# A two-layer block on one core: the end of the embedding gate, the blockwise inverse and the leads of one feed-forward are changed

## The chip, the cores and the metric

The kernel runs on one core of a Trainium2 chip. The metric is the device time of one execution in microseconds (us); lower is better. A core has five engines that each work through a queue of their own in order: TensorE (PE, matrix products and transposes), VectorE (DVE), ScalarE (ACT), GpSimd (POOL) and SyncE (SP, here the issuer of nearly all loads). They meet through semaphores. SBUF is the working memory, PSUM the memory of eight banks into which PE writes.

## The reference

The input is 256 tokens of 1024 columns. A first block of two layers is followed by a second block of two. The changed parts lie in the first block, and at the output of the second:

```python
def swiglu(x, w_in, w_out):
    gate, up = jnp.split(x @ w_in, 2, axis=-1)
    return (jax.nn.silu(gate) * up) @ w_out
...
    # token_mix, delta rule in chunks of 64 tokens, 4 heads
    m = jnp.where(strict, jnp.einsum('nbhik,nbhjk->nbhij', k_beta, k) * decay, 0.0)
    eye = jnp.eye(CHUNK, dtype=m.dtype)
    t_inv = lax.linalg.triangular_solve(eye + m, jnp.broadcast_to(eye, m.shape),
                                        left_side=True, lower=True)
    u = jnp.einsum('nbhij,nbhjv->nbhiv', t_inv, v * beta[..., None])
    w = jnp.einsum('nbhij,nbhjk->nbhik', t_inv, k_beta * jnp.exp(gcum)[..., None])
...
    # first_block
    for i in range(DEPTH):
        x = layer_norm(ALPHA * x + 0.5 * swiglu(x, ffn_w_in[i, 0], ffn_w_out[i, 0]), ln_g[i, 0], ln_b[i, 0])
        mix = token_mix(x, mix_w_in[i], ...)
        x = layer_norm(ALPHA * x + mix, ln_g[i, 1], ln_b[i, 1])
        x = layer_norm(ALPHA * x + 0.5 * swiglu(x, ffn_w_in[i, 1], ffn_w_out[i, 1]), ln_g[i, 2], ln_b[i, 2])
        ple = jax.nn.sigmoid(x @ ple_w_gate[i] + ple_b_gate[i]) * (p[i] @ ple_w_proj[i])
        x = layer_norm(ALPHA * x + ple, ln_g[i, 3], ln_b[i, 3])
```

There are 16 inverses of 64x64 in each layer (4 chunks of 64 tokens, 4 heads). The second block ends each of its layers with a product by `w_out` and a layer norm.

## The kernel before

**Products.** All data are fp32. A product is made of three on PE: high by high, high by low, low by high, where the high part is the operand rounded on ACT and the low part is the rest. Weights come in chunks of 1024 columns through six raw buffers (`raw`); ACT rounds a chunk into one of eight buffers `WH` (L312), then DVE or POOL subtracts and writes the low part `rawL` (L315). `round_chunk` and `pump` put these steps into the queues of ACT, DVE and POOL at the place in the program where they are called, so the order of the code is the order of the queues; a chunk used as an operand is asked for five chunks ahead. The activations, two halves of 128 tokens (t = 0, 1), are normalised rows `xt`, which PE turns (L597) into PSUM; ACT rounds them to `xTH` and DVE subtracts to `xTL` (`ln_split`).

**Phases.** Each layer of the first block goes through `ffn`, `mix`, `ffn`, `ple`. Each phase is a generator: `end_phase` runs the last product of one phase, its layer norm, and lets the generator of the next (`next(nxt)`) start its first products on half 0 (the *lead* units: their chunks hold four k of 256 columns, 12 tile products of 128x256, or two k of 512 columns) while half 1 is still being normalised.

**The end of a phase.** `by_tokens` makes the last product in steps of one k and one piece of columns: first three k for all pieces, then the rest of each piece. `inside` holds what is emitted ahead of a step: rounding and splits (`splits`), the layer norm of half 0 (`norm`) and its transposes (`turn`). For `ple` the second half has three pieces (512, 256 and 256 columns), 24 steps, and the sums and statistics follow piece by piece. The steps of `inside` are written by hand:

```python
inside = {0: norm, 6: splits} if not slow else {6: lambda: (splits(), norm())}
inside.update({first: lambda: turn(0, 0, x0), first + 1: lambda: turn(0, 1, x0)})
```

`slow` is set by `ple` alone, with `first` = 18; ACT must load a table of functions for the sigmoid and one for the square root of the layer norm (L334).

**The inverse** in `mix`: U, the inverse of 16 blocks, and its transpose T are built in five levels from masked blocks B of the matrix (`Bs`, masks made on POOL). A level makes Z = B U (products U, B in the trace), then U -= T-products and T -= Z-products:

```python
p = pe([Z_ready[t], T_ready[t], free], blocks(t, b, T, Z))
U_ready[t] = tt(half(U, t), half(U, t), half_ps(b, t), ALU.subtract, [p])
```

`blocks` walks over the blocks with two of the array's 64x64 quadrants in turn. Between these short products `go(n)` puts pieces of the next weight product on PE (12 tile products of 128x256 each), and `aside_` the convolution (`conv_steps`), `decayed_q`, `k_tokens` and `v_tokens`, which work on DVE and partly with transposes on PE (L1256). The products by the finished inverse follow (L1359 and what is behind it); the latter half of those walks over four quadrants in turn.

Of the kernel before, what the change touches and what calls it, by code (L numbers as in the profile page):

```python
# [24 lines left out]
S = 256  # L25
# [16 lines left out]

PHASES = [p for l in range(DEPTH) for p in (("ffn", l, 0), ("mix", l), ("ffn", l, 1), ("ple", l))]
# [5 lines left out]
def weight_units(phases):  # L49
# [14 lines left out]
    for ph in phases:  # L64
        l = ph[1]
        if ph[0] == "ffn":
            j = ph[2]
            for f in range(2):
# [3 lines left out]
            for f in range(2, NF):  # L72
# [173 lines left out]
def program(nc, io, phases=PHASES):  # L246
# [253 lines left out]

    def by_tokens(us, ks, t, aH, aL, a_ready, first, end, free, inside={}, place=None):
# [25 lines left out]
    def row_product(keys, order, aH, aL, a_ready, after={}):  # L527

        nu = len(order) // 2
        free = [bank_free[b] for b in range(4, 8)]  # L530
        for g in range(nu - LAST):
            u = Unit(keys + (g,))
            for i in range(2):
                k, first = order[2 * g + i], g == 0 and i == 0

                def fn(e, u=u, i=i, k=k, first=first):
                    for t in range(2):
                        for n in range(2):
                            e.matmul(PS[:, 4 + 2 * t + n, :], aH(k, t), u.H(i, 512 * n, 512), start=first, stop=False)  # L539
                            e.matmul(PS[:, 4 + 2 * t + n, :], aH(k, t), u.L(i, 512 * n, 512), start=False, stop=False)  # L540
                        for n in range(2):
                            ins = e.matmul(PS[:, 4 + 2 * t + n, :], aL(k, t), u.H(i, 512 * n, 512), start=False, stop=False)  # L542
# [6 lines left out]
        return lambda t, inside={}: by_tokens(us, order[2 * (nu - LAST):], t, aH, aL, a_ready, nu == LAST, True, free, inside)  # L549
# [10 lines left out]

    quarters_at = [None]
    quarter = [None]
# [45 lines left out]
    def add_acc(per):  # L608

        def fn(t, n, tok):  # L610
            yn, b = xt[:, t, 512 * n:512 * n + 512], 4 + 2 * t + n
            return stt(PS[:, b, :], yn, ALPHA * per, PS[:, b, :], ALU.mult, ALU.add, [tok, xt_loaded])
        return fn

    def end_phase(products, total, eps, nxt, first=9, slow=False):
# [9 lines left out]
        if nxt is None:  # L625
            x0 = ln_apply(0, stats, eps)
            last = products(1)
            x1 = ln_apply(1, [ln_stats(1, n, total(1, n, last[n, 0])) for n in range(2)], eps)
            for t, xs in ((0, x0), (1, x1)):
                for n in range(2):  # L630
# [27 lines left out]
        inside = {0: norm, 6: splits} if not slow else {6: lambda: (splits(), norm())}  # L658
        inside.update({first: lambda: turn(0, 0, x0), first + 1: lambda: turn(0, 1, x0)})
# [20 lines left out]
        for n in range(2):  # L680
# [3 lines left out]
            pump(st["split"])  # L684
# [7 lines left out]
    def ffn(l, j, nxt, start):  # L692
# [4 lines left out]
        sl, hl_ = take(f"sl{l}{j}", [128, 2, 2, 128]), take(f"hl{l}{j}", [128, 2, 2, 128])  # L697

        us = [Unit(("ffn_lead", l, j, f)) for f in range(2)]
        lead_h = {}
        lead_bank = {}
        lead_tok = {}

        def lead(t, f, c):
            if t not in lead_bank:
                lead_bank[t] = bank("A")
            b, free = lead_bank[t]
            n = KD // len(us[f].k)  # L710

            def fn(e):
                for q in range(n):
                    k = n * c + q
                    ins = mm3_moving(e, PS[:, b, 256 * f:256 * f + 256], xTH[:, k, 128 * t:128 * t + 128], xTL[:, k, 128 * t:128 * t + 128],
# [1446 lines left out]
```

How the kernel before makes its waits and increments, by code:

```python
    def play(self, handle, name):  # L222
        seen = {}
        for waits, fn, sem, inc in self.entries[name]:
            for s, v in waits:
                if seen.get(s.name, 0) < v:
                    seen[s.name] = v
                    handle.wait_ge(s, v)
            ins = fn(handle)
            if sem is not None:
                ins.then_inc(sem, inc)
# [1849 lines left out]
        @block.sync  # L2081
        def _(e):
            Q.play(e, "sync")
            e.wait_ge(sem_out, Q.loads[sem_out.name])
```

## Time and profile before

| | us |
|---|---|
| median of 3 runs | 1531.83 (1531.14 to 1532.82) |
| the profiled execution | 1531.08, its span 1529.3 |
| PE busy in the span | 1510.0 (99%) |
| DVE / ACT / POOL busy | 958.5 / 810.3 / 238.9 |
| mean granted clock of PE | 0.996 |
| read from HBM | 263.46 MB, 173 GB/s |

The span runs from the first to the last instruction that the profiler shows. Busy shares are means over stages of very different kinds: which engine sets the time has to be read at each place, from what PE waits for there. A clock of 1.00 is 2.4 GHz, 0.50 is 1.2 GHz.

### The profile page before, as it was taken

Reading aid. Unit: us, or ns where it says so; the run is one execution under the profiler, and the core shown is the slowest. Engines: PE = TensorE matmul, PEld = TensorE weight load, DVE = VectorE, ACT = ScalarE, POOL = GpSimd, SP = SyncE. Lnnn points to the kernel's source line nnn. Section 1 sums busy time; section 2 is a strip of 40 time slices with the busy share of each in tenths; the row PEclk is TensorE's granted clock in tenths of the full one; section 3 lists DMA queues with packets and bytes.
Section 4 is the critical chain, followed back from the end, with each engine's and each line's share of the span. In section 5 each row is a group of like instructions: output and inputs, shape, how many; then the busy total and the mean of one; then the engine's idle time right before and its main releaser. Section 6 shows DMA issues by size and latency. Waiting matters only on the chain.

```text
span 1529.3 us, 27766 instructions
## 1 busy us (share of the span) xinstructions
PE 1510.0 (99%) x11812; PEld 1396.0 (91%) x11812; DVE 958.5 (63%) x1389; ACT 810.3 (53%) x1249; POOL 238.9 (16%) x135
## 2 busy tenths in 40 slices
PE   9999999999999999999999999999999999999997
PEld 8998899989998879998899989998779999899996
DVE  6555476676555466654558685655476766767756
ACT  6544375545544355544574554544465675555762
POOL 0000242113000240000431040000420004500041
PEclk9999999999999999999999999999999999999999
DMA  9655463136555456555543155555455334553341
GB/s 384 220 193 193 166 221 130 66 111 224 190 193 193 165 203 217 193 193 193 196 164 112 56 175 211 193 193 192 165 184 190 136 115 161 206 194 138 118 159 56
DMA packets 39579, 266.30 MB, mean 174 GB/s; under 512 B 4444, under 2 KB 4444, under 8 KB 9248
## 3 DMA queue, kind: packets, MB, share of 16 engines
q1 hardware_dynamic: 38160, 260.13, 47.8%
q0 software_dynamic: 720, 3.35, 0.5%
q8 instruction: 94, 1.54, 0.4%
q10 hardware_dynamic: 576, 1.05, 0.2%
q14 instruction: 29, 0.24, 0.0%
HBM read 263.46 MB, written 1.05 MB: 173 GB/s over the span
## 4 chain that ended last, share of the span: by engine, by line
PE 94%; DVE 3%; ACT 1%; DMA 0%; issue 0%; POOL 0%; SPq 0%; DVEq 0%
PE PS L483 17%; PE PS L484 17%; PE PS L485 17%; PE PS L497 6%; PE PS L499 6%; PE PS L498 6%; PE PS L539 4%; PE PS L542 4%; PE PS L540 4%; PE PS L1270 2%; PE PS L466 1%; PE PS L467 1%; PE PS L468 1%; PE PS L1850 1%; PE PS L597 1%; DVE rawL L315 1%
## 5 line engine op out<-in xcount | busy, mean ns | idle before, releaser
L483 PE MATMUL PS<-xTH,WH 128*128 128x256 f32 x2272 | 645.8, 284 | 0.0
L484 PE MATMUL PS<-xTL,WH 128*128 128x256 f32 x2272 | 633.2, 279 | 0.0
L485 PE MATMUL PS<-xTH,rawL 128*128 128x256 f32 x2272 | 631.1, 278 | 0.0
L312 ACT ACTIVATE WH<-raw 128x1024 fp32r<-128x1024 f32 (+2 forms) x476 | 484.2, 1048 | 127.4 <-PE PS L542 101.3
L315 DVE TENSOR_TENSOR rawL<-raw,WH 128x1024 fp32r<-128x1024 f32 (+1 forms) x400 | 488.5, 1249 | 98.0 <-ACT WH L312 97.7
L483 PEld LDWEIGHTS PS<-xTH,WH 128*128 128x128 f32 x2272 | 426.7, 188 | 9.2 <-issue 6.7
L484 PEld LDWEIGHTS PS<-xTL,WH 128*128 128x128 f32 x2272 | 426.5, 188 | 3.4 <-issue 2.9
L485 PEld LDWEIGHTS PS<-xTH,rawL 128*128 128x128 f32 x2272 | 428.1, 188 | 0.0
L315 POOL TENSOR_TENSOR rawL<-raw,WH 128x1024 fp32r<-128x1024 f32 (+1 forms) x76 | 184.4, 2447 | 1069.1 <-ACT WH L312 1069.1
L312 ACT ACTIVATE sg<-PS 128x256 f32<-128x256 f32 x80 | 30.7, 384 | 182.4 <-PE PS L485 182.4
L315 DVE TENSOR_TENSOR hh<-PS,sg 128x256 f32<-128x256 f32 x80 | 33.9, 424 | 147.5 <-ACT sg L312 147.5
L539 PE MATMUL PS<-WH,hTH 128*128 128x512 f32 x256 | 100.7, 393 | 0.0
L540 PE MATMUL PS<-rawL,hTH 128*128 128x512 f32 x256 | 100.4, 392 | 0.0
L497 PE MATMUL PS<-WH,xTH 128*128 128x256 f32 (+2 forms) x272 | 89.2, 328 | 4.8 <-DVE rawL L315 2.4
L498 PE MATMUL PS<-rawL,xTH 128*128 128x256 f32 (+2 forms) x272 | 86.3, 317 | 0.0
L499 PE MATMUL PS<-WH,xTL 128*128 128x256 f32 (+2 forms) x272 | 86.2, 317 | 0.0
L542 PE MATMUL PS<-WH,hTL 128*128 128x512 f32 x256 | 79.9, 393 | 0.0
L318 DVE SCALAR_TENSOR_TENSOR PS<-xt,PS 128x512 f32<-128x512 f32 (+1 forms) x42 | 28.2, 671 | 61.9 <-PE PS L499 61.1
L497 PEld LDWEIGHTS PS<-WH,xTH 128*128 128x128 f32 x272 | 51.8, 191 | 10.9 <-ACT xTH L312 3.2
L315 DVE TENSOR_TENSOR hTL<-hh,hTH 128x256 fp32r<-128x256 f32 x80 | 34.1, 426 | 38.8 <-ACT hTH L312 38.8
L542 PEld LDWEIGHTS PS<-WH,hTL 128*128 128x128 f32 x256 | 48.1, 188 | 11.0
L539 PEld LDWEIGHTS PS<-WH,hTH 128*128 128x128 f32 x256 | 48.1, 188 | 10.8
(357 smaller groups left out, 2009.4 us busy)
## 6 DMA issues: line engine op xcount, KB each, us to landing
raw<-in_weights SPq DMA_DIRECT2D x233, 1024.0 KB, 4.8
gb<-in_lngb SPq DMA_DIRECT2D x16, 512.0 KB, 5.4
raw<-in_weights SPq DMA_DIRECT2D x2, 1056.0 KB, 4.9
gb<-in_ln SPq DMA_DIRECT2D x4, 512.0 KB, 4.3
cst<-in_consts POOLq DMA_DIRECT2D x1, 1378.5 KB, 10.3
raw<-in_weights SPq DMA_DIRECT2D x4, 256.0 KB, 5.4
x0T<-in_xT ACTq DMA_DIRECT2D x4, 256.0 KB, 5.7
xt<-in_x POOLq DMA_DIRECT2D x1, 1024.0 KB, 16.6
```

What stands on the lines that cost most here:

```text
L312: return Q.put("act", waits, lambda e: e.activation(out, in_, func, **kw))
L315: return Q.put(eng, waits, lambda e: e.tensor_tensor(out, a, b, op))
L483: e.matmul(out, c, xTH[:, k, :], start=k == 0, stop=False)
L484: e.matmul(out, c, xTL[:, k, :], start=False, stop=False)
L485: ins = e.matmul(out, u.L(i, 128 * k, 128), xTH[:, k, :], start=False, stop=k == KD - 1)
L497: e.matmul(out, aH, u.H(i, c0, w), start=first, stop=False)
L498: e.matmul(out, aH, u.L(i, c0, w), start=False, stop=False)
L499: return e.matmul(out, aL, u.H(i, c0, w), start=False, stop=end)
L539: e.matmul(PS[:, 4 + 2 * t + n, :], aH(k, t), u.H(i, 512 * n, 512), start=first, stop=False)
L540: e.matmul(PS[:, 4 + 2 * t + n, :], aH(k, t), u.L(i, 512 * n, 512), start=False, stop=False)
L542: ins = e.matmul(PS[:, 4 + 2 * t + n, :], aL(k, t), u.H(i, 512 * n, 512), start=False, stop=False)
L1270: ins = e.matmul(PS[R, b, 64 * i:64 * i + 64], lhsT[R, i, :], rhs[R, i, :], start=True, stop=True)
```

## The change

It has five parts.

1. **End of the embedding gate** (`end_phase` with `slow`): ACT's table for the square root is loaded ahead of rounding; rounding and splits are emitted ahead of steps 3, 6 and 9, not at step 6 alone; half 0's transposes stand ahead of steps 14 and 16, not 18 and 19. In layer one (`extra`) the table for half 1 and another round of splits on POOL come ahead of the first lead products, and later splits go to POOL too.
2. **Third lead unit** in layer two's first feed-forward (`lead_units`): three units instead of two run ahead, both halves of the third share a bank (`third_tok`, `third_act`), and its activations need two more transposes (`hl3`).
3. **First products of the program** (`lead_parts`): on half 0 each of the three products by parts waits for its own operand only.
4. **The inverse**: T is no longer updated with products; each level turns U with four full transposes (`flip`) and copies the result to T on DVE. Products of Z and of U run over the four quadrants in turn into two banks (`quadrants`); U is updated in two strided halves.
5. **End of the program**: the last row product of half 1 is made in three pieces (512, 256, 256), summed and normalised piece by piece; half 0 is stored as soon as it is ready, and the last stores are of 256 columns.

The core of the diff (allocation and renaming of the bank bookkeeping cut):

```diff
+def lead_units(l, j):
+    return 3 if l > 0 and j == 0 else 2
...
-    def row_product(keys, order, aH, aL, a_ready, after={}):
+    def quarters(where):
+        quarters_at[0] = where
+        quarter[0], free = bank("A")
+        return {(0, 0, 512): PS[:, 6, :], (1, 0, 256): PS[:, 7, 0:256], (1, 256, 256): PS[:, quarter[0], 0:256]}, free
...
-    def end_phase(products, total, eps, nxt, first=9, slow=False):
+    def end_phase(products, total, eps, nxt, first=(9, 10), slow=False, extra=False):
...
-            x0 = ln_apply(0, stats, eps)
+            def store(t, c0, w, tok):
+                src, dst = xt[:, t, c0:c0 + w], io["out"][128 * t:128 * t + 128, c0:c0 + w]
+                Q.dma("sync", [tok], sem_out, lambda e: e.dma_start(dst, src))
+            for n, tok in enumerate(ln_apply(0, stats, eps)):
+                store(0, 512 * n, 512, tok)
             last = products(1)
-            x1 = ln_apply(1, [ln_stats(1, n, total(1, n, last[n, 0])) for n in range(2)], eps)
-            for t, xs in ((0, x0), (1, x1)):
-                for n in range(2):
-                    src = xt[:, t, 512 * n:512 * n + 512]
-                    dst = io["out"][128 * t:128 * t + 128, 512 * n:512 * n + 512]
-                    Q.dma("sync", [xs[n]], sem_out, lambda e, src=src, dst=dst: e.dma_start(dst, src))
+            y = total(1, 0, last[0, 0])
+            stats = [ln_stats(1, 0, y, part) for part in range(2)]
+            stats += [ln_stats(1, 1, total(1, 1, last[1, 256 * part], c0=256 * part, w=256), part) for part in range(2)]
+            x1 = ln_apply(1, stats, eps)
+            store(1, 0, 512, x1[0])
+            for part in range(2):
+                store(1, 512 + 256 * part, 256, x1[1][part])
             return
+        if slow:
+            table(TBL_SQRT)
...
-        inside = {0: norm, 6: splits} if not slow else {6: lambda: (splits(), norm())}
-        inside.update({first: lambda: turn(0, 0, x0), first + 1: lambda: turn(0, 1, x0)})
+        inside = {0: norm, 6: splits} if not slow else {3: splits, 6: lambda: (splits(), norm()), 9: splits}
+        inside.update({first[0]: lambda: turn(0, 0, x0), first[1]: lambda: turn(0, 1, x0)})
...
             quarter_sum(0)
             pump(st["split"], "pool", lead=0)
             quarter_sum(1)
+            if extra:
+                table(TBL_SQRT)
+                pump(st["split"], "pool", lead=0)
...
-            pump(st["split"])
+            pump(st["split"], "pool" if extra else None)
...
+            key, col = (t, 256 * f) if f < 2 else ("third", 256 * t)
...
+            w, x = us[f].ready(c, 0), xT_ready[t][n * c // 4]
+            if start and t == 0:
+                tok = lead_parts(us[f], f, c, n, w, x, PS[:, b, 256 * f:256 * f + 256], free)
+            else:
+                tok = pe([w, x, free], fn)
+            (lead_tok if f < 2 else third_tok)[t] = tok
...
+        def lead_parts(u, f, c, n, w, x, out, free):
+            toks = []
+            for part in range(3):
+                def fn(e, part=part):
+                    for q in range(n):
+                        k = n * c + q
+                        a, b = (xTL if part == 1 else xTH)[:, k, 0:128], (u.L if part == 2 else u.H)(c, 256 * q, 256)
+                        ins = e.matmul(out, a, b, start=part == 0 and k == 0 and f == 0, stop=part == 2 and k == KD - 1 and f == 1)
+                    return ins
+                toks.append(pe([[w[0], x[0], free], x[1], w[1]][part], fn))
+            return toks[-1]
...
+        def third_act():
+            b, _ = lead_bank["third"]
+            v = PS[:, b, :].rearrange("p (t g s) -> p t g s", t=2, g=2)
+            s = act(sl3[:, :, :], v[:, :, 0, :], ACT.Silu, [third_tok[0], third_tok[1]])
+            lead_h[2] = tt(hl3[:, :, :], v[:, :, 1, :], sl3[:, :, :], ALU.mult, [s])
+            release(b, lead_h[2])
...
-            for f, c in ((0, 0), (0, 1), (1, 0)):
+            for f, c in ((0, 0), (0, 1), (1, 0)) + (((1, 1),) if nl == 3 else ()):
...
-            lead(0, 1, 1)
+            lead(0, *((2, 0) if nl == 3 else (1, 1)))
...
+        if nl == 3:
+            lead(0, 2, 1)
...
+                if nl == 3:
+                    b, free = bank("A")
+                    def fn(e, b=b):
+                        for t in range(2):
+                            ins = e.transpose(PS[:, b, 128 * t:128 * t + 128], hl3[:, t, :], ident)
+                        return ins
+                    p = pe([lead_h[2], free], fn)
+                    h_ready[2] = split(hTH[:, 2, :], hTL[:, 2, :], PS[:, b, 0:S], [p])
+                    release(b, h_ready[2])
...
-        end_phase(products, total, "eps5x4", nxt, 18, True)
+        end_phase(products, total, "eps5x4", nxt, (14, 16), True, l + 1 < DEPTH)
...
+        def quadrants(bs, lhsT, rhs, back):
+            def fn(e):
+                for m in range(4):
+                    for a_, odd in ((0, 0), (1, 1), (0, 1), (1, 0)):
+                        i, c, R, O = 2 * m + odd, 2 * m + a_, slice(64 * a_, 64 * a_ + 64), slice(64 * odd, 64 * odd + 64)
+                        out, src, j, b = (R, O, c, bs[odd]) if back else (O, R, i, bs[a_])
+                        ins = e.matmul(PS[out, b, 64 * m:64 * m + 64], lhsT[src, j, :], rhs[src, j, :], start=True, stop=True)
+                return ins
+            return fn
+        def flip(b, x):
+            def fn(e):
+                for m in range(4):
+                    ins = e.transpose(PS[:, b, 128 * m:128 * m + 128], x[:, 2 * m:2 * m + 2, :].rearrange("p i s -> p (i s)"), ident)
+                return ins
+            return fn
...
-        T_ready = [tt(half(T, t), eye, half(Bs[0], t), ALU.subtract, [b_ready[0]]) for t in range(2)]
...
         for n in range(1, 6):
             B = Bs[n % 2]
+            b, free = bank("B")
+            p = pe([U_ready, free], flip(b, U))
+            T_ready = copy(T[:, :, :], PS[:, b, :].rearrange("p (i s) -> p i s", i=8), [p])
+            release(b, T_ready)
             zb_ = [bank("B") for _ in range(2)]
+            p = pe([b_ready[n], U_ready, [free for _, free in zb_]], quadrants([b for b, _ in zb_], B, U, False))
             Z_ready = []
-            for t in range(2):
-                b, free = zb_[t]
-                p = pe([b_ready[n], U_ready[t], free], blocks(t, b, B, U))
-                Z_ready.append(act(half(Z, t), half_ps(b, t), ACT.Copy, [p]))
-                release(b, Z_ready[t])
+            for k, (b, _) in enumerate(zb_):
+                Z_ready.append(act(every2(Z, k), every2_ps(b), ACT.Copy, [p]))
+                release(b, Z_ready[k])
             b_free[n % 2] = p
             if n + 2 < 6:
                 level_mask(n + 2)
             go(1)
             if n == 5:
                 v_tokens(1)
-            for t in range(2):
-                b, free = bank("B")
-                p = pe([Z_ready[t], T_ready[t], free], blocks(t, b, T, Z))
-                U_ready[t] = tt(half(U, t), half(U, t), half_ps(b, t), ALU.subtract, [p])
-                release(b, U_ready[t])
-                if n < 5:
-                    b, free = bank("B")
-                    p = pe([free], blocks(t, b, Z, T))
-                    T_ready[t] = tt(half(T, t), half(T, t), half_ps(b, t), ALU.subtract, [p])
-                    release(b, T_ready[t])
+            ub = [bank("B") for _ in range(2)]
+            p = pe([Z_ready, T_ready, [free for _, free in ub]], quadrants([b for b, _ in ub], T, Z, True))
+            for k, (b, _) in enumerate(ub):
+                U_ready[k] = tt(every2(U, k), every2(U, k), every2_ps(b), ALU.subtract, [p])
+                release(b, U_ready[k])
```

On ACT's queue at the end of layer one's embedding gate, from the sigmoids of half 0 on (`PS<-PS` are the sigmoids, `lnsd` the square root, `xTH` half 0's rounded rows, `WH` weight chunks), stood before:

```order
L312 ACTIVATE PS<-PS 128x512 x2
L312 ACTIVATE WH4_64<-raw5_59 128x1024
L312 ACTIVATE WH5_65<-raw5_59 128x1024
L334 ACT_TABLE_LOAD
L312 ACTIVATE lnsd_78<-lnmv_77,cst_49 128x1
L334 ACT_TABLE_LOAD
L312 ACTIVATE xTH_52<-PS 128x4x128
L312 ACTIVATE PS<-PS 128x512
L312 ACTIVATE xTH_52<-PS 128x4x128
L312 ACTIVATE PS<-PS 128x256
L312 ACTIVATE WH6_66<-raw0_54 128x1024
L312 ACTIVATE PS<-PS 128x256
```

and stand now:

```order
L316 ACTIVATE PS<-PS 128x512 x2
L338 ACT_TABLE_LOAD
L316 ACTIVATE WH4_64<-raw5_59 128x1024
L316 ACTIVATE WH5_65<-raw5_59 128x1024
L316 ACTIVATE lnsd_78<-lnmv_77,cst_49 128x1
L338 ACT_TABLE_LOAD
L316 ACTIVATE WH6_66<-raw0_54 128x1024
L316 ACTIVATE xTH_52<-PS 128x4x128
L316 ACTIVATE PS<-PS 128x512
L316 ACTIVATE xTH_52<-PS 128x4x128
L316 ACTIVATE PS<-PS 128x256
L316 ACTIVATE WH7_67<-raw0_54 128x1024
```

The first table load has moved ahead of two roundings, and `WH6` ahead of half 0's rows; `WH7` now stands between the sigmoids, where `WH6` stood.

On PE at the same place, where half 1's first transposes (`cst,xt`, the identity and the rows) come between lead products, stood before:

```order
L497 MATMUL PS<-WH6_66,xTH_52 128x256
L498 MATMUL PS<-rawL0_68,xTH_52 128x256
L499 MATMUL PS<-WH6_66,xTL_53 128x256
L597 MATMUL PS<-cst_49,xt_51 128x128 x4
L497 MATMUL PS<-WH7_67,xTH_52 128x256
L498 MATMUL PS<-rawL0_68,xTH_52 128x256
L499 MATMUL PS<-WH7_67,xTL_53 128x256
```

and stand now:

```order
L501 MATMUL PS<-WH7_67,xTH_52 128x256
L502 MATMUL PS<-rawL0_68,xTH_52 128x256
L503 MATMUL PS<-WH7_67,xTL_53 128x256
L614 MATMUL PS<-cst_49,xt_51 128x128 x4
L501 MATMUL PS<-WH0_60,xTH_52 128x256
L502 MATMUL PS<-rawL1_69,xTH_52 128x256
L503 MATMUL PS<-WH0_60,xTL_53 128x256
```

The transposes now stand behind the chunk `WH7`, and the next chunk, `WH0`, is the third unit's.

On DVE in the inverse of layer one, from the U of level 1 to that of level 2, stood before (`cva` are convolution steps, `eb` belongs to `decayed_q`):

```order
L315 TENSOR_TENSOR U0_109<-U0_109,PS 128x256
L315 TENSOR_TENSOR T0_108<-T0_108,PS 128x256
L315 TENSOR_TENSOR U0_109<-U0_109,PS 128x256
L315 TENSOR_TENSOR T0_108<-T0_108,PS 128x256
L315 TENSOR_TENSOR rawL3_71<-raw3_57,WH4_64 128x1024
L318 SCALAR_TENSOR_TENSOR cva0_94<-PS,par_50,cva0_94 128x255 x2
L318 SCALAR_TENSOR_TENSOR cva0_94<-PS,par_50,cva0_94 128x254 x2
L315 TENSOR_TENSOR eb0_100<-eb0_100,kq0_93 128x512
L315 TENSOR_TENSOR U0_109<-U0_109,PS 128x256
```

and stand now, from the copy of level 1 to that of level 2:

```order
L328 COPY T0_110<-PS 128x512
L319 TENSOR_TENSOR U0_111<-U0_111,PS 128x4x64 x2
L319 TENSOR_TENSOR rawL3_71<-raw3_57,WH4_64 128x1024
L322 SCALAR_TENSOR_TENSOR cva0_96<-PS,par_50,cva0_96 128x255 x2
L322 SCALAR_TENSOR_TENSOR cva0_96<-PS,par_50,cva0_96 128x254 x2
L319 TENSOR_TENSOR eb0_102<-eb0_102,kq0_95 128x512
L328 COPY T0_110<-PS 128x512
```

The four halves of U and T have become one copy ahead of two strided halves of U; the second copy stands behind split, convolution and `eb`.

## Rows read from the trace of the kernel before

**Rows 1.** The page: the chain that ended last, by engine

```profile
PE 94%; DVE 3%; ACT 1%; DMA 0%; issue 0%; POOL 0%; SPq 0%; DVEq 0%
```

**Rows 2.** Windows, PE alone: stretch, us, busy, rows, clock, DMA share, GB/s

```profile
562.24:572.32 10.08, 7.10 (x59) 1.00 0.79 317
572.32:578.05 5.73, 5.73 (x52) 1.00 0.72 219
1120.57:1127.94 7.37, 5.22 (x24) 1.00 0.95 389
1127.94:1134.85 6.91, 6.05 (x17) 0.51 0.54 183
1134.85:1137.86 3.01, 3.01 (x14) 1.00 0.19 27
```

**Rows 3.** Timeline, layer one's embedding end: start, length, engine, operation, [idle <-releaser]

```profile
559.24 0.60 PE L597 MATMUL PS<-cst,xt 128*128 128x128 f32 x4
...
559.60 0.36 PE L497 MATMUL PS<-WH,xTH 128*128 128x256 f32 x1
...
560.51 0.69 DVE L315 TENSOR_TENSOR xTL<-PS,xTH 128x512 fp32r<-128x512 f32 x1 [1.48 <-ACT xTH L312]
...
561.67 1.05 ACT L312 ACTIVATE WH<-raw 128x1024 fp32r<-128x1024 f32 x1
...
563.01 1.28 ACT L334 ACT_TABLE_LOAD   x1
...
566.35 0.26 DVE L576 BATCH_NORM_AGGREGATE lnmv<-lnq 128x2 f32<-128x24 f32 x1
...
567.97 2.35 POOL L315 TENSOR_TENSOR rawL<-raw,WH 128x1024 fp32r<-128x1024 f32 x1 [2.77 <-ACT WH L312]
...
568.72 0.66 PE L597 MATMUL PS<-cst,xt 128*128 128x128 f32 x4 [1.77 <-DVE xt L318]
...
570.47 0.36 PE L497 MATMUL PS<-WH,xTH 128*128 128x256 f32 x1 [1.09 <-POOL rawL L315]
```

**Rows 4.** Timeline, layer two's embedding end

```profile
1127.04 0.66 PE L597 MATMUL PS<-cst,xt 128*128 128x128 f32 x4 [1.80 <-DVE xt L318]
```

**Rows 5.** Windows, layer one's inverse: PE, weight load, DVE, ACT, POOL; clock, DMA, GB/s

```profile
255.33:287.55 32.22, 32.22 (x585) 30.09 (x584) 24.44 (x45) 11.55 (x22) 4.98 (x6) 1.00 0.27 97
```

**Rows 6.** Chain, layer one's inverse: start, length, engine, line, rows

```profile
258.06 2.01 PE PS L1270 x64
...
293.33 0.62 PE PS L1359 x32
```

**Rows 7.** Timeline, layer one's inverse and just behind it, PE, DVE and POOL

```profile
261.59 1.65 DVE L318 SCALAR_TENSOR_TENSOR cva<-PS,par,cva 128x255 f32<-128x255 f32 x4
...
262.86 1.30 POOL L315 TENSOR_TENSOR Ba<-Es,cst 128x512 f32<-128x512 f32 x1 [4.99 <-PE PS L1270]
...
263.15 1.55 DVE L315 TENSOR_TENSOR eb<-eb,kq 128x512 f32<-128x512 f32 x1
...
264.99 0.42 DVE L315 TENSOR_TENSOR U<-U,PS 128x256 f32<-128x256 f32 x1 [0.28 <-PE PS L1270]
...
266.73 1.22 DVE L315 TENSOR_TENSOR rawL<-raw,WH 128x1024 fp32r<-128x1024 f32 x1
...
267.76 0.60 PE L1256 MATMUL PS<-cst,kq 128*128 128x128 f32 x4
...
268.29 1.15 PE L1270 MATMUL PS<-U,Bb 64*64 64x64 f32 x32
...
269.37 0.38 PE L483 MATMUL PS<-xTH,WH 128*128 128x256 f32 x1
...
297.50 0.68 DVE L324 COPY Sa<-PS 128x512 f32<-128x512 f32 x1
```

**Rows 8.** Timeline, the program's start

```profile
5.66 1.13 ACT L312 ACTIVATE WH<-raw 128x512 fp32r<-128x512 f32 x2
...
7.23 0.36 PE L497 MATMUL PS<-WH,xTH 128*128 128x256 f32 x1 [1.77 <-DVE rawL L315]
```

More of the change, by code:

```diff
@@ L67, in weight_units @@
             j = ph[2]
-            for f in range(2):
+            for f in range(lead_units(l, j)):
                 n = 4 if units else 2
@@ L71, in weight_units @@
                                                        for kt in range(n * c, n * c + n)] for c in range(KD // n)]))
-            for f in range(2, NF):
+            for f in range(lead_units(l, j), NF):
                 tile_unit(("ffn_in", l, j, f), "ffn_w_in", (l, j), t(128 * f), t(DFF + 128 * f))
@@ L499, in mm3_moving @@
         return e.matmul(out, aL, u.H(i, c0, w), start=False, stop=end)
+    quarters_at = [None]
+    quarter = [None]
     def by_tokens(us, ks, t, aH, aL, a_ready, first, end, free, inside={}, place=None):
@@ L525, in program, with row_product @@
     LAST = 3
-    def row_product(keys, order, aH, aL, a_ready, after={}):
+    def quarters(where):
+        quarters_at[0] = where
+        quarter[0], free = bank("A")
+        return {(0, 0, 512): PS[:, 6, :], (1, 0, 256): PS[:, 7, 0:256], (1, 256, 256): PS[:, quarter[0], 0:256]}, free
+    def row_product(keys, order, aH, aL, a_ready, after={}, quarters_in=None):
         nu = len(order) // 2
         free = [bank_free[b] for b in range(4, 8)]
+        place = None
+        if quarters_in is not None:
+            place, freeq = quarters(quarters_in)
+            free.append(freeq)
         for g in range(nu - LAST):
@@ L537, in fn @@
                     for t in range(2):
-                        for n in range(2):
[L539 to L542, printed above, removed]
+                        pieces = {(n, 0, 512): PS[:, 4 + 2 * t + n, :] for n in range(2)}
+                        if t == 1 and place:
+                            pieces = place
+                        for (n, c0, w), out in pieces.items():
+                            e.matmul(out, aH(k, t), u.H(i, 512 * n + c0, w), start=first, stop=False)
+                            e.matmul(out, aH(k, t), u.L(i, 512 * n + c0, w), start=False, stop=False)
+                        for (n, c0, w), out in pieces.items():
+                            ins = e.matmul(out, aL(k, t), u.H(i, 512 * n + c0, w), start=False, stop=False)
                     return ins
@@ L548, in row_product @@
         us = [Unit(keys + (nu - LAST + q,)) for q in range(LAST)]
-        return lambda t, inside={}: by_tokens(us, order[2 * (nu - LAST):], t, aH, aL, a_ready, nu == LAST, True, free, inside)
+        return lambda t, inside={}: by_tokens(us, order[2 * (nu - LAST):], t, aH, aL, a_ready, nu == LAST, True, free, inside, place if t else None)
     aside = []
@@ L697, in ffn @@
         sl, hl_ = take(f"sl{l}{j}", [128, 2, 2, 128]), take(f"hl{l}{j}", [128, 2, 2, 128])
-        us = [Unit(("ffn_lead", l, j, f)) for f in range(2)]
+        sl3, hl3 = take(f"sl3{l}{j}", [128, 2, 128]), take(f"hl3{l}{j}", [128, 2, 128])
+        nl = lead_units(l, j)
+        us = [Unit(("ffn_lead", l, j, f)) for f in range(nl)]
         lead_h = {}
@@ L747, in ffn @@
             for c in range(2):
-                for f in range(2):
+                for f in range(nl):
                     lead(1, f, c)
@@ L751, in ffn @@
         lead_act(1)
+        if nl == 3:
+            third_act()
         h_ready = {}
         h_tok = {}
-        for f in range(2, NF):
+        for f in range(nl, NF):
             u = Unit(("ffn_in", l, j, f))
@@ L833, in ple @@
         bgR, *bias_ready = ple_bias[l]
-        quarters_at[0] = at(f"lnq{l}", [128, 4, 6], F32, over + PLE_AT + 13 * 1024)
+        lnq = at(f"lnq{l}", [128, 4, 6], F32, over + PLE_AT + 13 * 1024)
         def aH(k, t):
```

36 lines of the change are left out of this document (19 added, 17 removed).

## Prediction

> **What bounds the kernel now.** The chain that ended last comes first [rows 1]: 94% of it is TensorE (PE). So a term counts only if it takes products or transposes off PE, or takes away time in which PE waits or runs slowly; what DVE, ACT and POOL save where PE never stops is worth nothing. The second view is a table of chosen stretches for PE alone, at the ends of the two embedding gates (ple) [rows 2]. Layer one: from the first lead product on token half 0 to the first unit on both halves, PE needs 10.08 us for 48 products of 128x256 and two sets of four transposes. The next stretch of 5.73 holds 48 products too (its 52 rows take in some that reach over its edges): 0.119 each, 0.36 for a step of three; a set of transposes takes 0.36 (559.24 to the next row at 559.60) [rows 3]. That is 6.4, so 3.65 us are lost. Layer two: 7.37 + 6.91 = 14.28 us for 30 products of 128x512, of which the row after shows 13 in 3.01 (0.232 each): 6.95 + 0.7, so 6.63 are lost. There the granted clock is 0.51 from 1127.94 on, the 1.2 GHz level, after PE had waited twice; 12 products and a set of transposes lie in it, 3.1 us of work at 2.4 GHz that took 6.05. So 2.9 of the 6.63 are clock, 3.7 waiting. The rows of the two ends name the waits: 1.77 and 1.80 for the normalised rows of token half 1 (xt), 1.09 for a low part of weights made on POOL [rows 3, 4]. In the block inverse, by contrast, PE is busy for all of 32.22 us in each layer [rows 5]: there it is work that must go, not waiting.
>
> **The embedding's end.** DVE works without a pause from the first split of half 0 (560.51) to the last aggregate (566.35 + 0.26), and the transposes of half 1's x follow at 568.72, 2.1 us later [rows 3]. The start of that DVE stretch hangs on half 0's transposes, which stand before step 18 of 24 (559.24). They move to step 14, four steps of 0.36 earlier, so the stretch starts 1.4 us sooner, and with it all that follows. Between 0 and 1.4 is possible, since the last quarter of half 1's gate cannot come sooner than its last product at 562.24; I take 1.4, because DVE has most of its work on the earlier pieces. The early table of half 0 takes a load of 1.28 off ACT's path, but PE did not wait there: nothing.
>
> Layer one: after the gate's last product there are now four lead chunks of 12 products (4 x 1.43 = 5.7) instead of three ahead of half 1's transposes: until 567.95, while x is there at 568.72 - 1.4 = 567.3. So the wait of 1.77 goes (bound: some of it stays, if x is late). Next come a chunk of the third unit (1.43), the other transposes, and its second chunk, wanted at 567.95 + 0.36 + 1.43 + 0.36 = 570.1. Low parts: the chunk that waited 1.09 is now rounded one slot earlier, so it has no wait. The third unit's first rounding follows a table load that ends at 563.01 + 1.28 = 564.3 and takes 1.05; then POOL has two splits of 2.35 in a row, to 570.1 [rows 3]. So 0.1 to 0.2 of waiting is left, and its two transposes on PE are new, some 0.2. Gain **3.3** (bounds: 1.9 if POOL is most of a split late, 3.6). The third unit's products are only moved.
>
> Layer two has no third unit. Its 18 lead products end at 1120.57 + 18 x 0.232 = 1124.75, x arrives at 1127.04 - 1.4 = 1125.6 (0.9 lost) [rows 2, 4], the last chunk now has its low part, and half 1's own splits behind the transposes I allow 0.5, most of a split of 0.69 [rows 3]. Loss 1.4 instead of 3.7, and no two long waits in a row, so I expect no fall of the clock: layer one had the same two waits and stayed at 1.00 [rows 2, 3]. Gain 2.3 + 2.9 = **5.2** (bounds: 2.3 with the fall kept, 6.0).
>
> **The inverse.** Before, a level costs PE 1.08 us for its first 16 products (two rows each in the trace) and 2.01 for the 32 others (T and U); the fifth level has 16 of those [rows 6, 7]. After, T is U turned by four full transposes and copied by DVE, and both sets of 16 go over four quadrants in turn. Products in just that order stand in the trace: 16 in 0.62 [rows 6]. Four transposes in this stage take 0.53 (267.76 to 268.29) [rows 7]. A level then costs 0.53 + 2 x 0.62 = 1.77. Sum: 4 x 3.09 + 2.16 = 14.5 before, 5 x 1.77 = 8.85 after, 5.7 us per layer if PE stays busy.
>
> But PE will not stay busy, because of who is in front of the T copy. It stands on DVE behind the previous level's U, the weight split and that level's aside work, and the second set of products waits for it. From rows [rows 7], level 1 to 2: two U 0.84, split 1.22, four convolution steps 1.65, one product on eb 0.68 (as the copy of 128x512; it took 1.55 beside POOL's mask), T copy 0.68; less 0.3, since each row starts a little before the one ahead ends: 4.8. Then PE's 0.62 and two hand-overs of 0.15: 5.7, and with part of eb's overlap 6.2. PE alone could do the level in two runs of twelve tile products (1.43, and 0.17 for the change of kind, as 0.53 against 0.36 shows for transposes) and 1.77, 4.97. Levels 2 to 3 (two steps, two passes of 0.68) and 3 to 4 (four steps, two passes) come to 5.6 and 6.4 in the same way, and 4 to 5 to 6.0, where PE with its own extra transposes is the longer. With 3.6 ahead of the first U and 1.4 behind the last: 29.2 against 32.22 [rows 5]. Gain 2.9 per layer, **5.8** (bounds: 0 per layer, if every level meets a busy DVE at the wrong moment; 5.7).
>
> POOL's mask lasts 1.30 in that stage [rows 7]; no row shows a copy from PSUM beside POOL. SBUF — State Buffer in the Trainium skill, section Who interferes with whom, says that DVE copies and GpSimd can shut each other out of the shared port for a whole instruction. By that rule one T copy per layer would wait for the rest of a mask, and the sum would be 2 x 0.6 smaller.
>
> **Start and end of the program.** The first product waits 1.77 us until a low part is done; in three parts, the first needs only ACT's rounded part, finished at about 6.2, half way through 5.66 + 1.13 [rows 8]. The whole chunk still needs the low part, so a chunk ends only about 0.5 sooner, and the next half's x is not earlier: gain **0.3** (0 to 0.6). At the end, the sum and the statistics of the last 512 columns become those of 256: passes of 0.42 instead of 0.68 [rows 7], two of them, **0.5** (0 to 1.0). The early stores and the smaller pieces in PE's last row product I put at nothing: PE takes 0.119 for 256 columns against 0.232 for 512.
>
> **Sum.** 3.3 + 5.2 + 5.8 + 0.3 + 0.5 = 15.1. The profiled execution took 1531.08, so 1516.0; its time is 0.75 below the median 1531.83, so I say **1516.7**.
>
> **Rivals.** (a) The clock still falls once, at an embedding's end or in the new inverse with its short waits: 2.9 to 3.4 worse, 1520. For it: two equal ends gave one fall and one not. Against: waits now much shorter. 0.15. (b) DVE is no limit in the inverse, because convolution steps slip into PE's longer stretches: 5.7 per layer, 1511. For it: DVE is busy 24.4 of 32.2 us there [rows 5]. Against: the order on its queue. 0.12. (c) The inverse gives nothing, T's copy returning all that the quadrants save: 1522.5. 0.10. (d) Slower than before: PE runs at 1.2 GHz in the inverse, where its work gets thinner and has waits in it. The 26.5 us of products per layer would double: 53 more, 1570 if in all of it. From 15 of those 53, when PE is at that level for more than three tenths of the stage, the change loses. Against: in the old inverse the clock is 1.00 throughout [rows 5]. 0.02. TensorE: Matmul & The Clock Gate in the Trainium skill, section Why this matters for your kernels, warns of idle gaps between bursts. (e) The change does not act at the ends: PE's waits belong to something else there, as the landing of weights; 1525 with the inverse alone. 0.03.
>
> **How the numbers follow.** My forecast has 0.58, with a range of its own of 1513.5 to 1519. To leave out no more than two in ten I take in (a), (b) and the near side of (c): **1511 to 1521.5**. What differs by less than 0.2% (3 us) cannot be told from no change here. Only (d) and far ends of (c) and (e) come near that: faster 0.95, same 0.03, slower 0.02.
>
> **What will show it.** Right: at both ends the waits of 1.77 to 1.80 shrink below 1.0 or vanish, and no stretch at half clock follows; sets of 32 small product rows at 0.62; the inverse's stretch at 29 us, with PE waits of about a microsecond ahead of the second set in the middle levels, and T's copy as the releaser. Wrong: a stretch of 26.5 (b) or of 32 (c); a granted clock of 0.5 inside the inverse (d); the sets over quadrants still at 1.08, which would take away 4.6 us of PE's saving per layer.

## The result and the profile after

| | before | changed |
|---|---|---|
| median, us | 1532.32 (1531.14 to 1533.93, 4 runs) | 1514.78 (1514.39 to 1514.95, 4 runs) |
| profiled execution, us | 1531.08 | 1514.83 |
| its span | 1529.3 | 1513.0 |

The ratio is 0.9886, with a 95% interval of 0.9872 to 0.9901: faster by 1.1%. The forecast was 1516.7, its range 1511 to 1521.5.

The page's chain that ended last, by engine, beside [rows 1]: PE still carries it.

```profile
PE 94%; DVE 4%; ACT 1%; DMA 0%; issue 0%; SPq 0%; DVEq 0%
```

The view of waits for PE says what is left (engine, line and what it waited for; us in total, times, longest):

```profile
PE PS L1351 <- DVE T L328: 4.3, 4, 1.1
PE PS L2131 <- DVE warm L2127: 1.2, 1, 1.2
PE PS L470 <- DVE mt L322: 0.7, 1, 0.7
PE PS L614 <- DVE xt L322: 0.7, 1, 0.7
```

The wait for T's copy (L328) is new, twice in each layer. At the embeddings' ends only one wait of 0.7 is left. The same view of the kernel before has 5.8 us there:

```profile
PE PS L597 <- DVE xt L318: 3.6, 2, 1.8
...
PE PS L497 <- POOL rawL L315: 2.2, 2, 1.1
```

The windows of the two ends, PE alone, columns as in [rows 2]. The first holds layer one's six lead chunks on half 0 (72 products) and the two sets of transposes; the other two hold layer two's 30 products and two sets:

```profile
557.98:567.41 9.43, 9.43 (x82) 1.00 0.92 356
1109.27:1114.32 5.05, 4.34 (x20) 1.00 0.88 371
1114.32:1118.30 3.98, 3.98 (x21) 1.00 0.88 363
```

Layer one's stretch is 9.43 us without idle time for 72 products (1.43 per chunk, 8.6) and two sets. Layer two's 14.28 are 9.03, and the clock is 1.00 throughout. The timeline at both ends shows why (rows between are left out):

```profile
554.84 0.69 DVE L319 TENSOR_TENSOR xTL<-PS,xTH 128x512 fp32r<-128x512 f32 x1 [1.00 <-ACT xTH L316]
...
560.68 0.26 DVE L593 BATCH_NORM_AGGREGATE lnmv<-lnq 128x2 f32<-128x24 f32 x1
563.64 0.60 PE L614 MATMUL PS<-cst,xt 128*128 128x128 f32 x4
...
1114.32 0.66 PE L614 MATMUL PS<-cst,xt 128*128 128x128 f32 x4 [0.71 <-DVE xt L322]
```

DVE's stretch is as long as before (554.84 to 560.94, 6.10 us; 560.51 to 566.61 in [rows 3]), but the last aggregate ends 3.0 us after the gate's last product (557.98) instead of 4.4: 1.4 sooner, as forecast.

In the inverse (all engines, columns as in [rows 5]) the stretch from the first transposes of U to the first product with v is

```profile
254.78:283.31 28.53, 26.39 (x479) 23.95 (x477) 22.27 (x40) 11.36 (x22) 4.96 (x6) 1.00 0.29 108
```

26.39 us of work, 2.13 of idle time. The timeline takes 0.69 for a set of 32 small rows and 1.15 for one of before [rows 7]; the chain's view, which the forecast's 0.62 and 1.08 come from, has a set begin 0.07 later. The timeline from the second set of level 1 to that of level 4, DVE, POOL and the second sets:

```profile
257.51 0.69 PE L1351 MATMUL PS<-Z,T 64*64 64x64 f32 x32
258.28 0.75 DVE L319 TENSOR_TENSOR U<-U,PS 128x256 f32<-128x256 f32 x2 [2.17 <-PE PS L1351]
258.95 1.22 DVE L319 TENSOR_TENSOR rawL<-raw,WH 128x1024 fp32r<-128x1024 f32 x1
260.08 1.65 DVE L322 SCALAR_TENSOR_TENSOR cva<-PS,par,cva 128x255 f32<-128x255 f32 x4
261.01 1.29 POOL L319 TENSOR_TENSOR Ba<-Es,cst 128x512 f32<-128x512 f32 x1 [3.60 <-PE PS L1351]
261.64 1.21 DVE L319 TENSOR_TENSOR eb<-eb,kq 128x512 f32<-128x512 f32 x1
262.77 0.68 DVE L328 COPY T<-PS 128x512 f32<-128x512 f32 x1
263.60 0.69 PE L1351 MATMUL PS<-Z,T 64*64 64x64 f32 x32 [1.14 <-DVE T L328]
...
267.49 1.29 POOL L319 TENSOR_TENSOR Bb<-Es,cst 128x512 f32<-128x512 f32 x1 [5.18 <-PE PS L1351]
268.13 0.68 DVE L328 COPY T<-PS 128x512 f32<-128x512 f32 x1
268.95 0.69 PE L1351 MATMUL PS<-Z,T 64*64 64x64 f32 x32
...
275.34 0.69 PE L1351 MATMUL PS<-Z,T 64*64 64x64 f32 x32 [0.99 <-DVE T L328]
```

DVE runs from 258.28 to 263.45 without a pause, and PE's second set starts 0.15 behind the copy.

Where the time went, by the starts of the same PE instructions in the two traces (each gain is the difference of the two stretches):

| stretch | forecast | measured |
|---|---|---|
| start, to the first product of q and k | 0.3 | 0.33 |
| layer one, inverse | 2.9 | 3.92 |
| layer one's end and layer two's first feed-forward | 3.3 | 3.13 |
| layer two, inverse | 2.9 | 3.93 |
| layer two's end | 5.2 | 5.22 |
| second block, up to its last row product | 0 | -0.76 |
| last row product and end | 0.5 | 0.49 |
| sum | 15.1 | 16.26 |

The sum is the difference of the two profiled executions' spans; the medians lie 17.5 apart.

### The profile page after: what moved, and what is told of

It is laid out like the page before. It is cut to its first block, busy times and chain, and to the rows that moved or that the text cites. A ratio compares the mean times of both kernels' runs of the same rounds, so it can differ in the third digit from the quotient of the medians.

```text
span 1513.0 us, 27372 instructions
## 1 busy us (share of the span) xinstructions
PE 1496.9 (99%) x11622; PEld 1384.2 (91%) x11622; DVE 947.8 (63%) x1379; ACT 811.1 (54%) x1249; POOL 250.5 (17%) x140
## 4 chain that ended last, share of the span: by engine, by line
PE 94%; DVE 4%; ACT 1%; DMA 0%; issue 0%; SPq 0%; DVEq 0%
PE PS L487 17%; PE PS L488 17%; PE PS L489 16%; PE PS L501 6%; PE PS L503 6%; PE PS L502 6%; PE PS L559 4%; PE PS L562 4%; PE PS L560 4%; PE PS L470 1%; PE PS L471 1%; PE PS L472 1%; PE PS L614 1%; PE PS L1942 1%; DVE rawL L319 1%; PE PS L1351 1%
## 5 line engine op out<-in xcount | busy, mean ns | idle before, releaser
L487 PE MATMUL PS<-xTH,WH 128*128 128x256 f32 x2256 | 641.2, 284 | 0.0
L319 DVE TENSOR_TENSOR rawL<-raw,WH 128x1024 fp32r<-128x1024 f32 (+1 forms) x395 | 481.4, 1245 | 102.5 <-ACT WH L316 102.2
L487 PEld LDWEIGHTS PS<-xTH,WH 128*128 128x128 f32 x2256 | 423.6, 188 | 9.2 <-issue 6.7
L319 POOL TENSOR_TENSOR rawL<-raw,WH 128x1024 fp32r<-128x1024 f32 (+1 forms) x81 | 196.1, 2443 | 1049.8 <-ACT WH L316 1049.8
L560 PEld LDWEIGHTS PS<-rawL,hTH 128*128 128x128 f32 x256 | 48.1, 188 | 10.7
```

The source lines that it names most:

```text
L319: return Q.put(eng, waits, lambda e: e.tensor_tensor(out, a, b, op))
L487: e.matmul(out, c, xTH[:, k, :], start=k == 0, stop=False)
L560: e.matmul(out, aH(k, t), u.L(i, 512 * n + c0, w), start=False, stop=False)
```

## The experiments

Each kernel is the changed one with one edit, beside runs of the kernel before on the same chip.

**1. The inverse of before.** The section from the first U to the end of a level is exchanged:

```diff
-            p = pe([U_ready, free], flip(b, U))
-            T_ready = copy(T[:, :, :], PS[:, b, :].rearrange("p (i s) -> p i s", i=8), [p])
...
+                    p = pe([free], blocks(t, b, Z, T))
+                    T_ready[t] = tt(half(T, t), half(T, t), half_ps(b, t), ALU.subtract, [p])
```

> All of the change except the inverse, which is that of before (T updated by products, two quadrants in turn). The theory: the new inverse gives 3.9 us in each layer, by how far the products ahead of it and behind it stand apart in the two traces, so this kernel takes 7.9 more than the changed one, about 1522.7, its stretch is 32.2 us again, and the ends of the two embeddings look as in the changed kernel. The rival: part of that shift comes from the neighbours (the next weights' low parts, the third lead unit), and this kernel costs less than 5 us more, under 1519.8.

Measured: 1522.21 (1521.62 to 1522.64), ratio 0.9945 (0.9931 to 0.9960); the stretch is 32.22 us again, and the ends look as in the changed kernel. So the inverse is worth 7.4 us by the medians (of runs on two chips) and 7.8 by the profiled executions; the rest of the change is worth 8.4, by the runs of the kernel before beside these (1530.61).

**2. T's copy on ACT.**

```diff
-            T_ready = copy(T[:, :, :], PS[:, b, :].rearrange("p (i s) -> p i s", i=8), [p])
+            T_ready = act(T[:, :, :], PS[:, b, :].rearrange("p (i s) -> p i s", i=8), ACT.Copy, [p])
```

> The changed kernel with the copy of T on ACT instead of DVE. The theory: the waits of 1.14 and 0.99 us ahead of the second set of products in levels 2 and 4 come from what stands ahead of the copy on DVE's queue (U, split, convolution, eb). On ACT only the previous rounding stands there, so these waits go: 2.1 us per layer, 4.3 in all, about 1510.5. The rival: the copy is late because the transposes are, or ACT's own copies of Z now come 0.6 later and take the same time back: within 1 us of the changed kernel, 1513.8 to 1515.8.

Measured: 1509.83 (1509.10 to 1510.18), ratio 0.9864 (0.9848 to 0.9881). The window of all engines over the same stretch:

```profile
254.93:281.12 26.19, 26.19 (x478) 23.87 (x477) 19.18 (x35) 14.14 (x27) 4.97 (x6) 1.00 0.32 118
```

No idle time on PE: the stretch is the PE work alone, 2.3 us shorter. The wait belonged to DVE's queue. The two versions were timed again side by side:

> The changed kernel as it is, beside the next one on the same chip: 1514.8, within 0.5, with the same waits of 0.95 to 1.14 in levels 2 and 4. All theories say so.

> The kernel with T's copy on ACT as it is, beside the changed kernel on the same chip. The theory of DVE's queue: 4.3 to 5 less than the changed kernel, 1510. The rival, that the first comparison owed part of its difference to two chips: less than 3 between them.

Measured: 1514.96 (1514.07 to 1515.46), ratio to before 0.9894 (0.9877 to 0.9911), and 1510.47 (1509.94 to 1510.64), ratio 0.9866 (0.9849 to 0.9882). 4.5 us apart: this version beats both.

**3. Half 0's transposes late again.**

```diff
-        end_phase(products, total, "eps5x4", nxt, (14, 16), True, l + 1 < DEPTH)
+        end_phase(products, total, "eps5x4", nxt, (18, 19), True, l + 1 < DEPTH)
```

> The changed kernel with half 0's transposes ahead of steps 18 and 19 again at both embeddings' ends; rounding ahead of steps 3, 6 and 9 stays. The theory: the start of DVE's stretch hangs on these transposes, so half 1's rows come 1.4 us later. In layer two the wait of 0.71 becomes 2.1 and the clock may fall again (2.9 more); in layer one the lead products end at the time the rows came before, and 1.3 of waiting comes back. Together 2.7 more, or 5.6 with the fall: 1517.5 or 1520.4. The rival: DVE waits for the last pieces of the gate anyway, and the place of the transposes is worth less than 0.5: 1514.8 to 1515.3.

Measured: 1517.39 (1516.52 to 1519.09), ratio 0.9916 (0.9901 to 0.9930). The timeline at both ends, and the window of PE behind the second:

```profile
564.60 0.65 PE L614 MATMUL PS<-cst,xt 128*128 128x128 f32 x4 [0.68 <-DVE xt L322]
...
1116.68 0.66 PE L614 MATMUL PS<-cst,xt 128*128 128x128 f32 x4 [2.13 <-DVE xt L322]
```

```profile
1116.68:1121.23 4.55, 4.54 (x17) 0.62 0.71 219
```

The wait of 0.71 is 2.13, as expected, and the clock falls behind it; layer one gets 0.68 where 1.3 was expected. By the traces layer one's end costs 0.87 more and layer two's 2.75, of which 1.42 are waiting; the rest, 1.3, is the fall, for which 2.9 was expected.

**4. Rounding ahead of step 6 alone.**

```diff
-        inside = {0: norm, 6: splits} if not slow else {3: splits, 6: lambda: (splits(), norm()), 9: splits}
+        inside = {0: norm, 6: splits} if not slow else {6: lambda: (splits(), norm())}
```

> The changed kernel with rounding and splits emitted ahead of step 6 alone, as before; the transposes stay at steps 14 and 16, the early table stays. The theory: the wait of 1.1 us for POOL's low part comes back in layer two, and in layer one each of the lead chunks' low parts is a slot later, so that one wait of 1 to 1.4 us stands there too: 2.2 more, 1517.0, more by 2.9 if the clock falls with it. The rival: POOL has time to spare once half 1's rows come sooner, and nothing changes: 1514.8.

Measured: 1517.90 (1517.69 to 1519.97), ratio 0.9921 (0.9906 to 0.9935). The timeline of PE at the two ends:

```profile
563.75 0.36 PE L501 MATMUL PS<-WH,xTH 128*128 128x256 f32 x1 [1.15 <-POOL rawL L319]
...
566.08 0.36 PE L501 MATMUL PS<-WH,xTH 128*128 128x256 f32 x1 [0.25 <-POOL rawL L319]
...
568.44 0.36 PE L501 MATMUL PS<-WH,xTH 128*128 128x256 f32 x1 [0.30 <-POOL rawL L319]
...
1116.63 0.65 PE L614 MATMUL PS<-cst,xt 128*128 128x128 f32 x4 [0.71 <-DVE xt L322]
1118.39 0.47 PE L501 MATMUL PS<-WH,xTH 128*128 128x512 f32 x1 [1.11 <-POOL rawL L319]
```

The waits for POOL return, 1.70 us in layer one, in three pieces where one of 1 to 1.4 was expected, and 1.11 in layer two. The kernel takes 3.1 more than the changed one, expected 2.2. The clock does not fall, after waits of 0.71 and 1.11 in the same place.

**5. Two lead units.**

```diff
-    return 3 if l > 0 and j == 0 else 2
+    return 2
```

> The changed kernel without the third lead unit in layer two's first feed-forward (two units, as elsewhere). The theory: with half 1's rows 1.4 us sooner, three lead chunks end at about 562.2 on the changed kernel's clock and the first half of the rows is there at 563.0, so a wait of 0.8 stands at layer one's end, less 0.2 for two transposes that fall away: 0.6 more, about 1515.4. The first rival: the third unit carries the whole cover at this end, the wait is 1.8 again and the time 1516.4. The second: it buys nothing, 1514.6.

Measured: 1514.38 (1513.49 to 1515.12), ratio 0.9892 (0.9877 to 0.9907): no loss to be seen. In the trace the wait is there:

```profile
563.38 0.66 PE L614 MATMUL PS<-cst,xt 128*128 128x128 f32 x4 [0.65 <-DVE xt L322]
```

but the same unit loop behind it (L487 and the two lines after it) ran faster in this execution. Windows of PE over that loop, first the changed kernel's, then this one's:

```profile
575.90:609.90 34.00, 34.00 (x290) 1.00 0.67 237
```

```profile
571.64:609.40 37.76, 37.76 (x336) 1.00 0.64 228
```

0.117 us per row against 0.112, at the same clock: over 336 products some 1.6 us, which hide the wait less the two transposes saved. The kernel before has two units too and yet the slower pace in this loop (39.76 us for 338 rows), so two units alone do not bring the faster one. The third unit's worth of 0.6 is neither shown nor refuted by the times.

**6. No quarters at the end.**

```diff
-                               quarters_in=put_at("lnqt", [128, 4, 6], 78.5) if nxt is None else None)
+                               quarters_in=None)
```

(with sums, statistics and the last store by 512 columns)

> The changed kernel with the last row product of half 1 in two pieces of 512 columns, its sum and statistics and its last store by 512 columns, as before; half 0 is still stored early. The theory: the short last piece gives 0.7 behind the last product (the traces show 7.25 against 8.0 us from the last sum to the end), and the products in three pieces cost PE 0.1 to 0.2: 0.5 more than the changed kernel, 1515.3. The rival: the products in pieces, or the bank that they take, cost PE the 0.7 us that the stretch ahead of the end lost, and this kernel takes the same time, 1514.5 to 1514.9.

Measured: 1514.19 (1513.83 to 1515.08), ratio 0.9892 (0.9877 to 0.9906). From the first row product to the end the traces show 30.38 before, 30.01 here, 29.89 in the changed kernel: the quarters give 0.12. Storing half 0 early moved nothing: its first store goes out 17.85 us behind the first row product in the kernel before and here. The other 0.37 is a pause of DVE that the kernel before has there and this one has not, in the same code (timelines of DVE, first before, then here; the rows of DVE ahead of these two stand equally far behind that first row product, within 0.01 us):

```profile
1524.64 0.75 DVE L318 SCALAR_TENSOR_TENSOR xt<-PS,lnrs,gb 128x512 f32<-128x512 f32 x1 [0.48 <-DVE PS L318]
```

```profile
1508.00 0.75 DVE L322 SCALAR_TENSOR_TENSOR xt<-PS,lnrs,gb 128x512 f32<-128x512 f32 x1
```

The 0.76 us that the stretch ahead lost do not come from the pieces, as the rival had it: the products of that stretch take 22.93 in the changed kernel and 22.15 here, but 22.15 also in runs 2 to 4, which have the pieces behind it.

**7. No parts at the start.**

```diff
-            if start and t == 0:
+            if False:
```

> The changed kernel without the three parts in the program's first products. The theory: 0.3 more, 1515.1, with the first product at 7.2 instead of 6.1 and the stages behind it 0.3 later. The rival: DVE's low parts set the pace of these products anyway, and the stages behind stand where they were.

Measured: 1514.60 (1514.02 to 1515.24), ratio 0.9893 (0.9876 to 0.9909). The first product starts at 7.11 instead of 6.08, but the first product of q and k at 244.97; in the profiled kernels that keep the parts that start lies between 244.48 and 245.03. So the 0.3 are not shown: executions differ by more.

**8. No early table.**

```diff
-        if slow:
-            table(TBL_SQRT)
         x0, got = [], {}
```

> The changed kernel without the table load ahead of the rounding at the embeddings' ends (the load comes where the square root needs it). The theory: nothing, since rounding ahead of step 3 leaves ACT time to load it, or half 0's rows are up to 1.28 later and still there before step 14: 1514.8. The rival: half 0's rows miss step 14, its transposes wait in the middle of the gate's last product, and each end loses up to 1.3: 1516 to 1517.4.

Measured: 1514.64 (1514.54 to 1514.76), ratio 0.9894 (0.9879 to 0.9908). The square root of half 0 starts 1.0 later (551.32 against 550.34), and its transposes at 553.61 against 553.57: nothing.

**9. Quadrants two at a time** (with T's copy on ACT, so that no wait is in the way).

```diff
-                for m in range(4):
-                    for a_, odd in ((0, 0), (1, 1), (0, 1), (1, 0)):
+                for m, a_, odd in [(m, a_, odd) for pair in (((0, 0), (1, 1)), ((0, 1), (1, 0))) for m in range(4) for a_, odd in pair]:
+                    if True:
```

> The kernel with T's copy on ACT, and the 16 products of each set in another order: first all eight of the two quadrants on the diagonal, in turn, then all eight of the other two. Products, banks and results are the same. The theory: what makes 16 products 0.62 instead of 1.08 us is that four quadrants come in turn, so each set takes 1.08 again; 10 sets in a layer, 0.46 each, 9.2 in both layers, 1519. The rival: the two banks or the larger group make it, the sets stay at 0.62, and the time is that of the kernel with the copy on ACT, 1509.8.

Measured: 1515.92 (1515.73 to 1516.12), ratio 0.9902 (0.9885 to 0.9919), 5.5 to 6.1 more than with four in turn. In the timeline a set takes 0.97, between the 0.69 of the changed kernel and the 1.15 of [rows 7]:

```profile
255.31 0.97 PE L1351 MATMUL PS<-U,Bb 64*64 64x64 f32 x32
```

The order makes most of the difference, the expected size was missed. The starts of the 32 rows of the first set, as the trace gives them, in ns from one to the next:

```
before: 6 100 7 52 6 52 7 51 7 52 6 52 7 51 7 52 6 52 7 51 7 52 6 52 7 51 7 52 6 52 7
changed: 7 6 7 87 6 7 7 38 7 6 7 38 7 7 6 39 6 7 7 38 6 7 7 38 7 7 6 39 6 7 7
run 9: 6 100 7 52 6 52 7 51 7 6 7 38 7 51 4 4 2 49 3 3 4 51 7 52 6 51 8 51 7 51 7
```

Every 58 ns a group starts: two rows before, four now, with one row for each quadrant. In run 9 a few rows of the second pair of quadrants start beside the last of the first (groups of four in the middle). So a set lasts as long as the groups that follow each other: 16 x 58 ns before, with 16 rows in line for each of two quadrants, and 8 x 58 now. Run 9 has 13 groups: 8 rows stand in line for each quadrant, but the second pair of quadrants joins only the last three groups of the first.

**10. Quadrants by bank.** The 0.18 us between run 9 and before could also have been the banks.

```diff
...
+                        ins = e.matmul(PS[R, zb_[a_][0], 64 * i:64 * i + 64], B[R, i, :], U[R, i, :], start=True, stop=True)
...
```

> All of the change, but the inverse of before, in which the first 16 products of a level (Z) now put the two quadrants in two banks of PSUM instead of one bank for each half; the same two quadrants come in turn, Z leaves PSUM by 64 partitions at a time, and the other 32 products of a level stay as they were. It looks at the 0.18 us that lie between the sets of the run in the other order and those of before. The theory: two quadrants in turn are slower when they write the same bank, so each of these five sets takes 0.90 instead of 1.08: 1.8 us less in both layers than the kernel with the inverse of before, about 1520.5. The rival: the bank does not matter, and these sets stay at 1.08.

Measured: 1521.96 (1521.12 to 1522.87), ratio 0.9941 (0.9917 to 0.9965), and the sets stay at 1.15 by the timeline:

```profile
255.13 1.15 PE L1405 MATMUL PS<-U,Bb 64*64 64x64 f32 x32
```

My theory of the bank fell, and the line of rows in a quadrant accounts for both runs. Four quadrants in turn in a single bank were not tried, so whether the four need their two banks is open.

## Why the prediction was right

**The ends.** Both mechanisms stand, each by its own run: the transposes' place (run 3) and the slot of the rounding (run 4). The sizes came out, 3.3 and 5.2 against 3.13 and 5.22. In layer two the wait that stays is 0.71, forecast 0.9, and the clock holds. Run 3 shows a fall behind one wait of 2.13, run 4 none behind 0.71 and 1.11. That the clock had fallen after PE "had waited twice" was read wrongly: it fell at 1127.94, and the second wait, of 1.10, ran from 1127.70 to 1128.80. Why layer one stays at 1.00 after 1.77 and 1.09 [rows 3] is open. How layer one's 3.13 divides is not shown: run 3 gives back 0.87 of it and run 4 2.10, the third unit's share is open (run 5), and the second table load and the further splits of `extra` were not taken out by themselves.

**The inverse.** The step "PE will not stay busy, because of who is in front of the T copy" is right: the waits stand in levels 2 and 4, with the copy as releaser, 1.14 and 0.99, and they go when the copy leaves DVE (run 2). The size was off, 3.92 per layer instead of 2.9. Second set to second set took 6.09, 5.35, 6.39 and 5.72 us, forecast 6.2, 5.6, 6.4 and 6.0: 0.65 in all. The ends of the stretch, 3.6 and 1.4 in the forecast, are 2.73 and 2.25, equal in sum. And the stage starts 0.23 sooner behind the first product of q and k, which the sum left out. The first T (`T_ready` from `Bs[0]`), 0.84 us on DVE, is gone there, but run 1, which has it again, starts its stage 0.13 sooner too, so the cause is not shown. Rival (b), a PE that never waits, is what run 2 shows; its place of 5.7 per layer is then 32.22 - 26.19 = 6.0.

The Trainium skill's page SBUF — State Buffer, section Who interferes with whom, names two rules: a DVE instruction in a mode with two ports contends with GpSimd, and one with at most one input in SBUF, outside these modes, does not. The trace agrees with the second for T's copy, which reads PSUM alone: the copy at 268.13 lies wholly beside the mask from 267.49 to 268.78 and takes 0.68, as it does without one (262.77). The prediction had put the copy under the first rule; the 2 x 0.6 that it priced were not lost. The product on `eb`, whose operands are in SBUF, took 1.21 where a mask ran beside it (261.64) and 0.68 where none did (273.91).

**Start and end.** The sums came out by luck (0.33 and 0.49), the reasons did not: the parts at the start are not shown by run 7, and of the end's 0.49 only 0.12 belongs to the quarters; 0.37 is DVE's pause in the profile of before, whose cause is open.

**What was not forecast** is the second block's -0.76, with no change in its code ahead of its last row product: the pace of PE's products there, 22.93 us against 22.15 before. It took back part of the 2.05 that the inverse gave beyond its forecast, so the total came out nearer than its terms.

**The other rivals.** (a) and (d): no fall of the clock, in the ends or in the inverse. (c): the inverse gave 7.85 of the 16.26. (e): runs 3 and 4 show the waits answering to the edits.

## What to carry to other kernels

Where an engine's queue is in order, a short copy on the path costs what stands ahead of it; walk that queue, and see which other engine has only work in front that is needed anyway: moving the copy was worth 4.5 us more. Small products that fill a quarter of the array should go over all four quadrants in turn, since rows of one quadrant line up: 16 products of 64x64 took 0.69 us here over four and 1.15 over two. A part of less than a microsecond can't be read from whole times that differ by as much between executions; compare the stretch, and check its pace of products first.

## What the runs showed of the hardware

**Two paces at one clock.** Products of 128x256 follow each other at 0.113 or at about 0.118 us, at a granted clock of 1.00, over tens of microseconds. In most places all profiles agree on which. In the unit loop of layer two's first feed-forward, run 5 had the faster pace from the start and the changed kernel the slower, until the transposes at 610 us. The products ahead of the last row product, the same code everywhere, take 22.92 to 22.93 in six of the profiles (the changed kernel among them) and 22.15 to 22.16 in the others and in the kernel before. The kernel with T's copy on ACT took 22.15 in its first profile and 22.93 in its second, so it is not the kernel that decides. What sets the pace is open.

**The clock's fall is not of one size.** In the kernel before it came 0.9 us behind the end of the wait of 1.80 [rows 4], while PE stood in the next wait, and lasted 6.83 us:

```profile
1128.80 0.77 PE L497 MATMUL PS<-WH,xTH 128*128 128x512 f32 x1 [1.10 <-POOL rawL L315]
```

In run 3 it came 1.1 us behind the end of a wait of 2.13, with PE busy, and lasted 3.41 us.
